# Later rounding of turned products, a strip cut from 512 to 296 columns, and compression steps in two breaks instead of eight

## Time and profile before

| what | value |
|---|---|
| runs | 1974.56, 1974.74, 1977.51 us |
| profiled execution | 1974.15 us, span of its instructions 1972.5 us |
| outside the span | 1.65 us |
| TensorE busy | 98% of the span |
| GpSimd busy | 81% |
| VectorE, ScalarE busy | 56%, 53% |
| mean granted clock | 0.992 |

### The profile page before, as it was taken

The page is one execution under the profiler, slowest core; times in us unless marked ns, Lnnn a source line. Parts: engine busy times, 40 slices in busy tenths (PEclk is TensorE's granted clock), DMA queues, the critical chain, the costliest instruction groups (busy, mean ns, idle before and its releaser), DMA issues.

```text
span 1972.5 us, 27090 instructions
## 1 busy us (share of the span) xinstructions
PE 1930.3 (98%) x9394; PEld 1555.1 (79%) x9394; DVE 1104.7 (56%) x2918; ACT 1041.5 (53%) x1762; POOL 1588.5 (81%) x1160
## 2 busy tenths in 40 slices
PE   8999999999999999999999999989999999998999
PEld 6888777888788877788877877777888777777787
DVE  5865545444545644544455776557555576646564
ACT  5445665544644566654475545544447554544543
POOL 6988876988698877598879687878888867785986
PEclk9999999999999999999999999999999999999999
DMA  6665434555665543467564333455657433345554
GB/s 218 239 212 174 167 120 150 192 192 194 209 223 194 181 160 118 165 197 257 194 249 156 126 131 119 138 175 203 221 182 269 141 136 129 119 149 171 171 192 139
DMA packets 98211, 348.66 MB, mean 177 GB/s; under 512 B 13436, under 2 KB 14108, under 8 KB 97820
## 3 DMA queue, kind: packets, MB, share of 16 engines
q1 hardware_dynamic: 97372, 345.80, 52.2%
q10 hardware_dynamic: 704, 1.14, 0.2%
HBM read 345.85 MB, written 1.05 MB: 176 GB/s over the span
## 4 chain that ended last, share of the span: by engine, by line
PE 86%; DVE 5%; ACT 5%; POOL 2%; issue 1%; DMA 0%; ACTq 0%; SPq 0%; DVEq 0%
PE psum L575 26%; PE psum L577 25%; PE psum L576 25%; DVE psum L1824 3%; POOL lo L548 2%; ACT hi L1269 1%; PE psum L744 1%; PE psum L645 1%; PE psum L767 1%; PE psum L754 1%; PE psum L977 1%; PE psum L734 1%; ACT big L1630 1%; DVE big L1811 1%; ACT big L1306 1%
## 5 line engine op out<-in xcount | busy, mean ns | idle before, releaser
L548 POOL TENSOR_TENSOR lo<-raw,hi 128x256 fp32r<-128x256 f32 (+1 forms) x1156 | 1588.3, 1398 | 369.8 <-ACT hi L1269 341.7
L1269 ACT ACTIVATE hi<-raw 128x1024 fp32r<-128x1024 f32 x616 | 643.2, 1057 | 400.9 <-PE psum L577 374.0
L575 PE MATMUL psum<-hi,h_hi 128*128 128x512 f32 x1632 | 654.0, 401 | 15.8 <-POOL lo L548 15.0
L577 PE MATMUL psum<-hi,h_lo 128*128 128x512 f32 x1632 | 639.3, 392 | 0.0
L576 PE MATMUL psum<-lo,h_hi 128*128 128x512 f32 x1632 | 638.4, 391 | 0.0
L1824 DVE STREAM_TRANSPOSE psum<-big 32x128 f32<-32x128 f32 x1216 | 392.5, 323 | 17.9
L575 PEld LDWEIGHTS psum<-hi,h_hi 128*128 128x128 f32 x1632 | 308.7, 189 | 89.3 <-POOL lo L548 21.0
L577 PEld LDWEIGHTS psum<-hi,h_lo 128*128 128x128 f32 x1632 | 307.6, 188 | 66.3
L576 PEld LDWEIGHTS psum<-lo,h_hi 128*128 128x128 f32 x1632 | 308.4, 189 | 60.1
L575 PE MATMUL psum<-hi,y_hi 128*128 128x512 f32 x832 | 331.5, 398 | 13.6 <-POOL lo L548 7.6
L576 PE MATMUL psum<-lo,y_hi 128*128 128x512 f32 x832 | 326.7, 393 | 0.0
(11 more groups left out here) (263 smaller groups left out, 1304.9 us busy)
## 6 DMA issues: line engine op xcount, KB each, us to landing
raw<-in_stream SPq DMA_DIRECT2D x616, 512.0 KB, 3.4
big<-in_w SPq DMA_DIRECT2D x14, 512.0 KB, 7.7
big<-in_post SPq DMA_DIRECT2D x6, 512.0 KB, 4.9
special<-in_b_merge SPq DMA_DIRECT2D x2, 1536.0 KB, 8.1
memkv<-in_mem SPq DMA_DIRECT2D x2, 1024.0 KB, 7.6
big<-in_band SPq DMA_DIRECT2D x2, 768.0 KB, 5.7
x<-in_x SPq DMA_DIRECT2D x2, 512.0 KB, 5.3
special<-in_special SPq DMA_DIRECT2D x2, 512.0 KB, 4.8
```

The costliest lines, as they stand in the source:

```text
L548: t = pool.tensor_tensor(M.lo[:, slot, w], M.raw[:, slot, w], f32(M.hi[:, slot_hi, w]), ALU.subtract)
L575: pe.matmul(out, lhs_hi, rhs_hi, start=start, stop=False)
L577: return pe.matmul(out, lhs_lo, rhs_hi, start=False, stop=stop)
L1269: act.activation(M.hi[:, slot_hi, :], M.raw[:, slot, :], ACT.Copy).then_inc(sem["hi"], 1)
```

## The change

1. **Order on ScalarE, gated stages.** The rounding of the turned product of strip s-1 comes after the rounding of stream piece c+7 instead of c+4.
2. **Order on ScalarE, second block's feed-forward.** Strip n0's comes after piece c+5 of `project(n0+2)` (it was inside `project(n0+1)`); strip n0+1's comes in the rows of n0, after the third of them (it was inside `project(n0+2)`); the later ones come after piece c+7; the last one after the second row piece instead of the first.
3. **Strip z3.** Its four pieces hold 2 x 296 columns instead of 2 x 512; DMA, ScalarE, GpSimd and TensorE work on those alone.
4. **Compression.** Steps 0 to 3 follow piece mq 1, steps 4 to 7 follow piece mv 1.

```diff
+WIDTH_Z3 = 296
-        "mk": (none, [prep[3]], none, [cmp[0], mem[0]]),
-        "mq": ([cmp[1], mem[1]], [cmp[2], mem[2]], [cmp[3], mem[3]], [cmp[4], mem[4]]),
-        "mv": ([mem[8], cmp[5], mem[5]], [cmp[6], mem[6]], [cmp[7], ("take_cmp",), mem[7]], [mu[0]]),
+        "mk": (none, [prep[3]], none, [mem[0]]),
+        "mq": ([mem[1]], cmp[0:4] + [mem[2]], [mem[3]], [mem[4]]),
+        "mv": ([mem[8], mem[5]], cmp[4:8] + [mem[6]], [("take_cmp",), mem[7]], [mu[0]]),
...
-        sp.dma_start(M.raw[:, slot, :], T["stream"][c]).then_inc(landed[slot], 16)
+        used = slice(0, 2 * half_width(c))
+        sp.dma_start(M.raw[:, slot, used], T["stream"][c][:, used]).then_inc(landed[slot], 16)
...
+def half_width(c):
+
+    at = (c - L * PIECES1) % PIECES2 if c >= L * PIECES1 else 0
+    z3 = 4 * STRIPS2.index("z3")
+    return WIDTH_Z3 if z3 <= at < z3 + 4 else PIECE // 2
...
-            w = slice(i * PIECE // parts, (i + 1) * PIECE // parts)
+            whole = 2 * half_width(c)
+            w = slice(i * whole // parts, (i + 1) * whole // parts)
...
+        cols = half_width(c)
...
-                w = slice(i * 512, i * 512 + 512)
-                t = product(psum[:, bank + m, :], a_hi[:, k, m * P:m * P + P], a_lo[:, k, m * P:m * P + P],
+                w = slice(i * cols, i * cols + cols)
+                t = product(psum[:, bank + m, 0:cols], a_hi[:, k, m * P:m * P + P], a_lo[:, k, m * P:m * P + P],
...
-        act.activation(M.hi[:, slot_hi, :], M.raw[:, slot, :], ACT.Copy).then_inc(sem["hi"], 1)
+        used = slice(0, 2 * half_width(c))
+        act.activation(M.hi[:, slot_hi, used], M.raw[:, slot, used], ACT.Copy).then_inc(sem["hi"], 1)
...
                 round_piece(c + j + AHEAD)
-                if j == 0 and s > n0:
+                if gated and j == 3 and s > n0:
                     turn(c, s - 1)
+                if not gated and j == (1 if s == n0 + 2 else 3) and s > n0 + 1:
+                    turn(c, n0 if s == n0 + 2 else s - 1)
...
                 round_piece(c + 4 + i + AHEAD)
+                if not gated and s == n0 + 2 and i == 2:
+                    turn(c, n0 + 1)
...
-                if i == 0:
+                if i == 1:
                     turn(c, n0 + strips - 1)
```

More of the change, by code:

```diff
@@ L2474, in pieces_of, with narrow_pieces @@
     return a.transpose(3, 0, 2, 1, 4).reshape(-1, P, PIECE)
+def narrow_pieces(w):
+    pairs = w.reshape(KD // 2, 2, P, WIDTH_Z3).transpose(0, 2, 1, 3).reshape(-1, P, 2 * WIDTH_Z3)
+    return np.pad(pairs, ((0, 0), (0, 0), (0, PIECE - 2 * WIDTH_Z3)))
 def ffn_pieces(up, down, strips, rows_per):
@@ L2507, in stream_of @@
         g = g.reshape(D, 2, 4, 3).transpose(0, 3, 2, 1).reshape(D, 24)
-        pad = np.zeros((D, 216), np.float32)
-        low = np.concatenate([vs, vw, g, gl, pad], 1)
+        low = np.concatenate([vs, vw, g, gl], 1)
         gqk = np.concatenate([gq, gk], 1)
@@ L2518, in stream_of @@
             m = i - STRIPS2.index("merge")
-            laid["strip", i] = pieces_of(mg[:, 512 * m:512 * m + 512] if name == "merge" else strips[name], 512)
+            laid["strip", i] = (narrow_pieces(low) if name == "z3" else
+                                pieces_of(mg[:, 512 * m:512 * m + 512] if name == "merge" else strips[name], 512))
         laid.update({("rows", b): pieces_of(rows_, 1024) for b, rows_ in ((2, wb[2]), (0, nsa_rows), (1, wb[1]))})
```

## The result

Four executions of the changed kernel took 1952.88, 1953.94, 1955.73 and 1955.79 us, median 1954.84, against 1974.65 for the kernel before, run beside them. The ratio is 0.9896, with a 95% interval of 0.9879 to 0.9913. The prediction was 1960 (1941 to 1970), most likely faster: right in direction and range, 5 us too slow. The profiled execution is the one of 1952.88 us, span 1951.2, the fastest of the four: its mean granted clock is 0.996, that of the others 0.992 to 0.994.

A forecast was written before the change was run, and what follows sets the result against it. The prediction took TensorE to bound the kernel, by its work and the waits before it. 1974.15 - 31.4 + 20 - 2 = 1960.7; three small gaps made 1959.6, the median's 0.6 made 1960 us, range 1941 to 1970.

The forecast's parts named there:

- Parts 1 and 2, removed: Feed-forward starts, first block's first layer and second block's both: TensorE's gaps and the slow clock behind them go, 31.4 us.
- The cover of 0.6 us: Second block's feed-forward: product of n0+2 ready near 1339.4, wanted by project(n0+3) near 1340.0, so 0.6 us left.
- Part 1, added: First feed-forward, gated strips with side work: later rounding delays the product; waits 13.3 us plus clock 6.7, 20 us added.
- the wait of 4 us behind strip 3: Layer 0's first feed-forward: sign of a new TensorE gap for VectorE's product at the start of strip 4, 4 us.
- The first: Side-work strips: old-trace durations (strip 2 5.1, strip 3 8.9 us) used for each; new waits 13.3 us in both layers.
- The second: Clock behind side-work waits: 1.7 us each for the 4.2 and two of 2.1, half for two of 1.65; 6.7.
- Parts 3 and 4: Second mixer: less TensorE work, but GpSimd bounds at mq 0; about 1.1 us a layer, 2.0 for both, bounds -2 to +12.
- the wait at mq 0: Second mixer, first piece of mq: TensorE waits 3.2 us for GpSimd in each layer, and the clock takes 1.7.
- part 4: Second mixer's compression: two blocks of four steps cost 4.2 us against 5.9, gain 1.7 a layer, bounds 0 and 2.5.
- A: Rival, first feed-forward: side work hides after all, added 5 us or less, 1945 (1935 if mixers give 12); chance 0.22.
- B: Rival: starts gain less as project(n0+3) waits for its product, side work costs 31 us; 1972.8, no change; chance 0.07.
- C: Rival, all 44 gated strips: late rounding makes every product late, 35 us more, 1996, slower; chance 0.05.
- D: Rival, mixers: after mq 0 further waits at mq 1 to 3, 3 us and clock a layer, 1969; chance 0.08.

The follow-up runs named there:

- experiment 2: Kernel before with the narrow strip alone (296 columns in place of 512 in the second mixer's third strip): 1974.43 us, ratio 1.0001.
- experiment 1: Kernel before with the two moves in ScalarE's order alone, strip and compression unchanged: 1957.0 us, ratio 0.9911.
- experiment 3: Kernel before with the compression's first steps put together in two breaks, alone: 1973.39 us, ratio 0.9996.
- experiment 5: Changed kernel with GpSimd in quarters on pieces 13 to 18 of the first feed-forward, beside the side work of strip 2: 1952.03 us, ratio 0.9887.
- experiment 6: Changed kernel with GpSimd making the four pieces of strip mk in the second mixer whole instead of in quarters: 1958.31 us, ratio 0.9917.
- experiment 8: Experiment 7 with the four pieces of mk made whole as in experiment 6: 1940.81 us, ratio 0.983.
- experiment 10: Experiment 7 with GpSimd in quarters on pieces 17 to 19 alone, beside the side work of strip 3: 1938.01 us, ratio 0.981.
- experiment 11: Experiment 7 with both the moved preparation of experiment 9 and the quarters of experiment 10: 1933.39 us, ratio 0.9788.
- experiment 7: Experiment 4 with VectorE's side work of the first layer (rotation angles) one strip later: 1939.33 us, ratio 0.9831.
- experiment 9: Experiment 7 with VectorE's two long scaling instructions moved from strip z3 behind mv's first piece, head rotation behind its third: 1933.87 us, ratio 0.979.
- experiment 4: Changed kernel with the first feed-forward's late rounding kept only for its second and third strip: 1946.75 us, ratio 0.9857.

## Why the prediction was right, and where its sizes were off

**What bounds the kernel** was read rightly: 8.6 us less work on TensorE gave nothing by itself (experiment 2), and waits gone gave 17.3 (experiment 1).

**Parts 1 and 2, removed: 31.4 us, right.** TensorE no longer waits at any of the five starts (their excess in the trace of before sums to 31.0 by the measure used here). The cover of 0.6 us before the product of n0+2 was 1.0 (the product ends at 1344.78, TensorE takes it at 1345.78). The three small gaps at other starts went too; they were worth 0.3 us each and not 0.4.

**Part 1, added: 20 us forecast, 14.2 found in the profiled execution.** This is the term that was mis-sized. By strips of layer 0, wait and clock together: strip 2, 1.1 forecast, 8.1 found; strip 3, 4.2 + 1.7 against nothing; strip 4, 0.5 against nothing; strip 8, 3.8 against 0.7; strip 9, 2.5 against 2.4. Layer 1: 3.8 and 2.5 against 0.7 and 2.4. Of its signs, the wait of 4 us behind strip 3 did not come, and one of 5.4 behind strip 2 did.

Two steps failed. The first: I worked out each strip alone, with the durations of the trace of before; but in strip 2 the side work had begun, at 48.40, while GpSimd had nothing to do (from 47.52 to 48.72, since ScalarE had stood at the turned product), and its first two instructions took 0.17 and 0.23 us; now all four met a busy GpSimd: 9.2 us in place of the 5.1 I used. The 5.1 was one draw even for the old order, as the traces of experiments 2 and 3 show (8.7 and 7.2). The wait that this made then covered strips 3 and 4. Experiment 5 shows that chain from the other end. In strip 8 the side work took 5.3 us in place of 6.7.

The second: I took slow clock behind the waits of some 2 us, 6.7 us in all. The waits in strips 8 and 9 (0.80 and 2.48 us long) had none behind them in the profiled execution. For the ones of 2.48 us that is chance: in the traces of the changed kernel and of experiments 1, 5 and 6 they occur eight times, and the clock fell behind three of them. So the prediction could have come nearer, or further off, by this alone.

The rule of the Trainium skill in the prediction ("SBUF — State Buffer", section "SBUF: two separate sides") is borne out by experiment 5: with a quarter of GpSimd's instruction to wait for, VectorE's took a fifth of the time. It also says that the one that starts first gets the ports and the other blocks for that instruction; experiment 8 goes beyond it, since the blocked one was passed over by six more.

**Parts 3 and 4: 2.0 us forecast, 2.3 found.** From piece 332 to 352 TensorE took 65.69 us in place of 67.19, and in the second layer 66.10 in place of 66.90. The narrow matmuls lie 0.137 us apart, as forecast; the wait at mq 0 is 2.81 and 3.21 (3.2 forecast), and the first piece of mq lasts 4.40 and 4.39 in place of 2.72, so the clock behind it took 1.7, as forecast. (The 32-column matmuls that bounded the price from below lie 0.112 apart and not 0.106, which changes nothing.) Not foreseen: a wait of 1.90 us before the windows' transposes (1.25 and 0.86 before). They stand behind the first narrow piece, so TensorE comes to them sooner, and they start only when VectorE's last rest of the memory features is done (1034.77 in the first layer). By this account it costs nothing on balance, since GpSimd bounds anyway; no run tests that. Four compression steps in a row add 1.96 us to the distance between two stream matmuls (0.66 + 3 x 0.43 = 1.95 forecast). That part 4 gives 1.7 us a layer of the kernel's time is not shown: experiment 3 can't tell it from nothing.

**Not in the sum at all: the clock behind old waits.** The wait before the first output piece of each second mixer (at 1242.40) is 2.4 us long before and after. Its excess was 3.84 and 3.86, and is 2.29 and 2.27 in the profiled execution of after: 3.1 us, the largest part of the error after the 5.8 of the term above. The order of work there is the same, so this too is how the clock fell in that execution, and no gain of the change. Against it stand two waits for GpSimd at 1279.95 and 1750.65 that rose from 0.7 to 1.57 us (1.7), and 0.6 at the beginning. 5.8 + 3.1 + 0.3 - 1.7 - 0.6 = 6.9, of the 6.7 between 1959.6 and 1952.88. The median of after lies 2 us above that execution, so part of what is explained here is its luck with the clock.

**The rivals.** A (the side work hides, 1945) was wrong for the changed kernel, but half true: it hides wherever GpSimd is starved. B, C and D are out; no strip without side work got a gap. The sum came near partly by luck: errors of 7 us in strip 2 and of 13 in the others stood against each other.

## What to carry to other kernels

Where two engines block each other, the duration of a small instruction is not its own: here it was about that of the other engine's instruction if that one had work (2.3 against 2.4 us), and 0.2 us if not. So removing a wait can lengthen side work near it, and a duration from the old trace holds only as long as the other engine's state there stays the same; go through the strips in order, with the new state of both. An order that helps at a stage's start can cost under side work later in the same loop: make it depend on the strip. And before shortening an engine's work, look at what sets the end there; here the narrow strip alone paid nothing. Moving two long instructions of VectorE out of the way then gave 5.5 us; how much of that is the narrow strip's is not shown, since no run has the move without it.

## What the runs showed of the hardware that was not expected

- A VectorE instruction that is kept out by GpSimd can be passed over by six of GpSimd's instructions in a row: 14.62 us for one that took 1.46 in another kernel's execution with the same order. That the other long execution (1946.18 against 1939.3) has this cause is only argued: it has no profile. With quarters that wait for one another (experiments 10 and 11) none of nine executions was long, but without them (7, 8 and 9) it was only two of thirteen, none of them in 9: that the quarters prevent it is not shown. What they do show is 2.0 us for the four small instructions together.
- Whether the granted clock falls behind a wait of 2.2 to 2.8 us differs from trace to trace, and between the two layers of one execution. The thirteen traces have 45 such waits (from one matmul to the next, the first 20 us left out): the clock fell behind 28 and not behind 17. In experiments 1, 9 and 10 the wait before the first output piece has slow clock behind it in one layer and none in the other. It fell behind all eleven waits of over 5 us and all seven of 3.2 to 3.3, behind seven of the nine of 3.6 to 4.3, and behind none of the 31 of 1.5 to 1.9. The same wait, with TensorE equally busy before it, in experiments 4 and 7; of the changed kernel it stands above with 1.00 and 18 matmuls:

```profile
1241.47:1247.47 6.00, 3.99 (x12) 2.84 (x11) 4.84 (x8) 3.12 (x11) 3.92 (x6) 0.78 0.32 112
```
```profile
1234.10:1240.10 6.00, 3.97 (x13) 2.87 (x12) 4.83 (x8) 3.13 (x11) 3.91 (x6) 0.80 0.30 109
```

  The excess is 3.88 and 3.89 here and 2.29 there, so 1.6 us more. In experiment 10 the waits of 2.79 and 2.81 us before mq had no slow clock behind them (3.48 and 3.36 of excess with the next short wait in it), where experiment 7 has 4.24 and 4.54. What decides between them stays open, so such a wait can be priced from these traces only with or without 1.6 us, and each kernel has one trace.
